# Gates, taps, conv tiles and output products at other items of the attention of two layers

## What is computed

```python
proj = einsum('bld,de->ble', h, w_in[l])
a, g, zc, q, k, v, za, qi, ki, wi = split(proj)
u = a * sigmoid(g)                          # 512 channels
u = depthwise_conv(u, w_dw, width=31) + b_dw
y_conv = silu(layer_norm(u, ln_g, ln_b)) * silu(zc)
y_attn = sparse_attention(q, k, v, qi, ki, wi, topk) * silu(za)   # 8 heads of 64
y = einsum('ble,ed->bld', concat([y_conv, y_attn]), w_out[l])
h = layer_norm(DEEPNORM_ALPHA * h + y, post_ln_g[l], post_ln_b[l])
```

## Time and profile before

| | us |
|---|---|
| median of three runs | 1079.3 (1077.6 to 1079.58) |
| the profiled execution's own time | 1078.45 |
| span of the profiled execution | 1076.7 |
| TensorE busy | 1002.7 |
| VectorE busy | 665.8 |
| ScalarE busy | 582.3 |
| GpSimd busy | 197.1 |

### The profile page before, as it was taken

One profiled execution on the slowest core, in us unless ns is written; L12 is line 12 of the kernel. 1 busy time (PEld: TensorE's weight loads), 2 busy tenths in 40 slices (PEclk: granted clock), 3 DMA queues, 4 the chain that ended last, 5 costly groups with the idle time before them and its releaser, 6 DMA issues.

```text
span 1076.7 us, 16592 instructions
## 1 busy us (share of the span) xinstructions
PE 1002.7 (93%) x6452; PEld 845.7 (79%) x6452; DVE 665.8 (62%) x1507; ACT 582.3 (54%) x944; POOL 197.1 (18%) x236
## 2 busy tenths in 40 slices
PE   6999999987899899999999787889999899999997
PEld 6998988864567799898887466778888778887885
DVE  3899999884673479999978645635631433332422
ACT  6585872555533458588255733444564656664321
POOL 0000661011211100077100302223200000000001
PEclk9999999996999999999999998989999999999999
DMA  7776873760202858487474610594777553547661
GB/s 286 184 175 197 192 175 111 186 155 24 58 1 80 189 149 193 118 186 172 117 179 109 156 36 1 157 232 120 185 172 210 137 118 96 140 122 152 156 157 79
DMA packets 23822, 152.36 MB, mean 142 GB/s; under 512 B 2865, under 2 KB 3377, under 8 KB 6849
## 3 DMA queue, kind: packets, MB, share of 16 engines
q0 software_dynamic: 9648, 68.75, 34.6%
q1 hardware_dynamic: 14096, 82.55, 21.4%
HBM read 149.20 MB, written 2.10 MB: 141 GB/s over the span
## 4 chain that ended last, share of the span: by engine, by line
PE 58%; DVE 21%; ACT 9%; issue 8%; DMA 3%; POOL 1%; POOLq 0%; DVEq 0%; SPq 0%; ACTq 0%
PE psum_B L1227 16%; PE psum_A L1260 7%; PE psum_A L1227 7%; PE psum_B L1260 6%; DVE score L1759 6%; DVE top L1750 5%; PE psum_A L1409 5%; DVE conv_acc L1704 4%; DMA w_lo<-in_weights 2%; PE psum_A L1620 2%; ACT w_hi L622 2%; PE psum_B L1620 2%; ACT w_lo L623 2%; PE psum_B L1409 1%; PE psum_B L1363 1%
## 5 line engine op out<-in xcount | busy, mean ns | idle before, releaser
L1704 DVE SCALAR_TENSOR_TENSOR conv_acc<-u,vec,conv_acc 128x528 f32<-128x528 f32 (+1 forms) x240 | 173.7, 759 | 3.2
L1041 POOL DMA_DIRECT2D w_lo<-in_weights x67 | 59.6, 889 | 605.5 <-ACT w_lo L623 579.1
L1227 PE MATMUL psum_B<-x_hi,w_hi 128*128 128x264 f32 (+3 forms) x512 | 144.2, 320 | 6.6 <-DVE mlp_lo L2129 3.6
L1227 PE MATMUL psum_B<-x_lo,w_hi 128*128 128x264 f32 (+3 forms) x512 | 141.6, 315 | 0.0
L1227 PE MATMUL psum_B<-x_hi,w_lo 128*128 128x264 f32 (+3 forms) x512 | 141.2, 314 | 0.0
L622 ACT ACTIVATE w_hi<-w_raw 128x2048 fp32r<-128x2048 f32 (+2 forms) x85 | 129.3, 1522 | 15.4 <-DMA w_raw<-in_weights 15.0
L623 ACT ACTIVATE w_lo<-w_raw 128x2048 fp32r<-128x2048 f32 (+2 forms) x85 | 128.7, 1514 | 0.0
L1227 PE MATMUL psum_A<-x_hi,w_hi 128*128 128x264 f32 (+2 forms) x496 | 115.9, 291 | 1.4 <-DVE x_lo L1911 1.0
L1227 PE MATMUL psum_A<-x_hi,w_lo 128*128 128x264 f32 (+2 forms) x496 | 113.8, 287 | 0.0
L1227 PE MATMUL psum_A<-x_lo,w_hi 128*128 128x264 f32 (+2 forms) x496 | 113.8, 287 | 0.0
L1227 PEld LDWEIGHTS psum_B<-x_hi,w_hi 128*128 128x128 f32 (+1 forms) x512 | 87.5, 185 | 16.2 <-issue 9.8
(11 more groups left out here) (339 smaller groups left out, 2175.6 us busy)
## 6 DMA issues: line engine op xcount, KB each, us to landing
w_raw<-in_weights SPq DMA_DIRECT2D x67, 1024.0 KB, 5.2
w_lo<-in_weights POOLq DMA_DIRECT2D x65, 1024.0 KB, 8.7
x_first<-in_x_t SPq DMA_DIRECT2D x4, 528.0 KB, 7.1
h<-in_x SPq DMA_DIRECT2D x1, 2048.0 KB, 10.8
out<-h SPq DMA_DIRECT2D x4, 512.0 KB, 2.6
post_ln_g<-in_post_ln_g SPq DMA_DIRECT2D x2, 512.0 KB, 3.8
post_ln_b<-in_post_ln_b SPq DMA_DIRECT2D x2, 512.0 KB, 5.3
w_raw<-in_weights SPq DMA_DIRECT2D x2, 288.0 KB, 5.3
```

What stands on the lines that cost most here:

```text
L1041: pool.dma_start(wlo[n % RING][:, 0:width], io["weights"][n, :, 0:width], accum_op=ALU.add) \
L1227: mm = pe.matmul(ps[0:cols, i, 0:b - a], w[wp][:, kt, at:at + cols], x[xp][:, kt, a:b], start=(kt == 0 and wp + xp == 0), stop=(kt == KD - ...
L1704: got = dve.scalar_tensor_tensor(dst, src, w, dst, ALU.mult, ALU.add)
```

## The change

All of it is in the tables and in the place of three operations. The gates keep their order, but items 4 and 6 have two of them, so that the twelve take ten items; the 38 taps take ten items as well. Conv tiles start two items earlier. The conv norm goes from DVE's extra work to a place of its own, between the masks and the scalings of the turn, and the affine step goes from item c + 3 to c + 4. Output products start at item 17 instead of 19, and some later ones move with them, as do both meta pairs, POOL's clearing of their buffer, post norms and splits. The squares' sums get other columns of a tile that becomes eight columns wide. The last products behind the tables (`OUTPUT_CONV_AT`) keep their items.

```diff
+GATE_ITEMS = (0, 1, 2, 3, 4, 4, 5, 6, 6, 7, 8, 9)
 CONV_AT = {
-    0: ((0, 12, "D", "C"), (1, 14, "B", "C"), (2, 16, "D", "C"), (3, 18, "B", "C"), (4, 20, "D", "C")),
+    0: ((0, 10, "D", "C"), (1, 12, "B", "C"), (2, 14, "D", "C"), (3, 16, "B", "C"), (4, 18, "D", "C")),
...
 OUTPUT_AT = {
-    0: ((19, 0, 0, "A"), (21, 0, 1, "B"), (24, 1, 0, "A"), (25, 1, 1, "B"), (27, 0, 2, "A"), (30, 1, 2, "A"),
+    0: ((17, 0, 0, "A"), (19, 0, 1, "B"), (23, 1, 0, "A"), (24, 1, 1, "B"), (27, 0, 2, "A"), (29, 1, 2, "A"),
         (35, 0, 3, "A")),
-    1: ((19, 0, 1, "A"), (21, 0, 2, "B"), (23, 1, 1, "A"), (25, 1, 2, "A"), (29, 0, 3, "A")),
+    1: ((17, 0, 1, "A"), (19, 0, 2, "B"), (21, 1, 1, "A"), (23, 1, 2, "A"), (27, 0, 3, "A")),
-META_AT = ((18, "attn"), (19, "conv"))
-POST_AT = {0: ((0, 26), (1, 30), (2, 34)), 1: ((1, 26), (2, 28))}
+META_AT = ((16, "attn"), (16, "conv"))
+POST_AT = {0: ((0, 26), (1, 28), (2, 34)), 1: ((1, 22), (2, 26))}
 SPLITS_AT = {
-    0: ((0, 1, ("zc", 2)), (2, 3, ("wo", 0, 0)), (6, 7, ("wo", 1, 0)), (10, 11, ("wo", 0, 1)), (19, 21, ("wo", 1, 1))),
-    1: ((0, 1, ("zc", 2)), (2, 3, ("wo", 0, 0)), (6, 7, ("wo", 1, 0)), (10, 11, ("wo", 0, 1)), (16, 18, ("wo", 1, 1))),
+    0: ((0, 1, ("zc", 2)), (2, 3, ("wo", 0, 0)), (5, 6, ("wo", 1, 0)), (8, 9, ("wo", 0, 1)), (19, 19, ("wo", 1, 1))),
+    1: ((0, 1, ("zc", 2)), (2, 3, ("wo", 0, 0)), (5, 6, ("wo", 1, 0)), (8, 9, ("wo", 0, 1)), (17, 17, ("wo", 1, 1))),
-TAPS_BY_ITEM = (3, 3, 3, 3, 3, 3, 3, 3, 4, 4, 3, 3)
+TAPS_BY_ITEM = (4, 3, 4, 3, 5, 4, 5, 4, 3, 3)
-        todo["dve"][i + 2].append(("norm", t))
+        todo["dve_early"][i + 2].append(("norm", t))
         todo["pe"][i + 3].append(("back", t, back))
-        todo["act"][i + 3].append(("affine", t))
+        todo["act"][i + 4].append(("affine", t))
-        todo["pool"][17].append(("clear", 0))
+        todo["pool"][14].append(("clear", 0))
...
                         masked_logits(l, i + 2)
                         masked_logits(l, i + 3)
+                        for op in early[i]:
+                            conv_norm(l, op[1])
                         normalise(l, i + 2)
                         normalise(l, i + 3)
```

More of the change, by code:

```diff
@@ L195 @@
 CONV_AT = {
-    0: ((0, 12, "D", "C"), (1, 14, "B", "C"), (2, 16, "D", "C"), (3, 18, "B", "C"), (4, 20, "D", "C")),
-    1: ((1, 12, "D", "C"), (2, 14, "B", "C"), (3, 16, "D", "C"), (4, 18, "B", "C")),
+    0: ((0, 10, "D", "C"), (1, 12, "B", "C"), (2, 14, "D", "C"), (3, 16, "B", "C"), (4, 18, "D", "C")),
+    1: ((1, 10, "D", "C"), (2, 12, "B", "C"), (3, 14, "D", "C"), (4, 16, "B", "C")),
 }
 OUTPUT_AT = {
-    0: ((19, 0, 0, "A"), (21, 0, 1, "B"), (24, 1, 0, "A"), (25, 1, 1, "B"), (27, 0, 2, "A"), (30, 1, 2, "A"),
+    0: ((17, 0, 0, "A"), (19, 0, 1, "B"), (23, 1, 0, "A"), (24, 1, 1, "B"), (27, 0, 2, "A"), (29, 1, 2, "A"),
         (35, 0, 3, "A")),
-    1: ((19, 0, 1, "A"), (21, 0, 2, "B"), (23, 1, 1, "A"), (25, 1, 2, "A"), (29, 0, 3, "A")),
+    1: ((17, 0, 1, "A"), (19, 0, 2, "B"), (21, 1, 1, "A"), (23, 1, 2, "A"), (27, 0, 3, "A")),
 }
-META_AT = ((18, "attn"), (19, "conv"))
-POST_AT = {0: ((0, 26), (1, 30), (2, 34)), 1: ((1, 26), (2, 28))}
+META_AT = ((16, "attn"), (16, "conv"))
+POST_AT = {0: ((0, 26), (1, 28), (2, 34)), 1: ((1, 22), (2, 26))}
 OUTPUT_CONV_AT = {0: 39, 1: 31}
@@ L236, in attention_extras @@
     n = len(attention_items(l))
-    todo = {engine: [[] for _ in range(n)] for engine in ("pe", "act", "dve_middle", "dve", "pool")}
+    todo = {engine: [[] for _ in range(n)] for engine in ("pe", "act", "dve_early", "dve_middle", "dve", "pool")}
     for gate in GATES_AHEAD[2:]:
         todo["dve"][0].append(gate)
-    for i, gate in enumerate(GATES_AT):
+    for i, gate in zip(GATE_ITEMS, GATES_AT):
         todo["pe"][i].append(gate)
@@ L371, in build @@
         nmax = sb("neg_max", [P, 4])
-        psums = sb("prob_sums", [P, 4])
+        psums = sb("prob_sums", [P, 8])
         rsums = sb("prob_rsums", [P, 4])
@@ L807, in squares @@
                     act.wait_ge(exp_made.sem, exp_made.at((2, "in", t - 1)))
-                act.activation(dst[:, :], h[:, t, :], ACT.Square, accum_out=psums[:, t - 1:t]) \
+                act.activation(dst[:, :], h[:, t, :], ACT.Square, accum_out=psums[:, t + 3:t + 4]) \
                     .then_inc(exp_made.mark((2, "in", t)), 1)
@@ L1082, in input_deviation @@
                 pool.wait_ge(exp_made.sem, exp_made.at((2, "in", t)))
-                reciprocal_deviation((2, "in", t), psums[:, t - 1:t], 1, P, 8 + t, 1.0 / D, EPS)
+                reciprocal_deviation((2, "in", t), psums[:, t + 3:t + 4], 1, P, 8 + t, 1.0 / D, EPS)
             pool.memset(u[:, :, 0:PAD], 0.0).then_inc(set_up.mark("pad"), 1)
@@ L1947, in _ @@
                 conv(l, 62, TAPS_AHEAD)
-                middle, todo = extras[l]["dve_middle"], extras[l]["dve"]
+                early, middle, todo = extras[l]["dve_early"], extras[l]["dve_middle"], extras[l]["dve"]
                 n = len(items[l])
@@ L1958, in woven @@
                             conv_stats(l, op[1])
-                        elif op[0] == "norm":
-                            conv_norm(l, op[1])
                         elif op[0] == "residual":
```

## The result

The changed kernel takes 1061.68 us (median of 4 runs, 1060.74 to 1063.52), the kernel before 1079.44 (1077.6 to 1082.58): the ratio is 0.9835, with a 95% interval of 0.9808 to 0.9862. The forecast was 1058, range 1047 to 1070. A second set of 6 runs gives 1061.72, ratio 0.9847 (0.9815 to 0.988). All ratios here are to the kernel before, in the same set. The span of the profiled execution goes from 1076.7 to 1059.4 us.

What follows compares the result with a forecast made beforehand. PE bounds the gate stages, a loop of waits across engines the conv stages; output stages hold idle PE and lost clock. Layer 0 gives -10.6, layer 1 -10.3, together -20.9 from 1078.45: 1057.5, said as 1058 us, range 1047 to 1070.

Steps and rivals of the forecast that it cites:

- the named waits: PE's waits: 5.60 us ahead of layer 0's first output product, 3.71 and 4.44 in layer 1's outputs; to shrink or go.
- Conv stages, -9.1 and -5.5: First conv transposes to first output product: 15.5 us instead of 24.60 in layer 0, 17.6 instead of 23.10 in layer 1.
- a loop in which no y and no affine is due yet: Conv stage loop of mask, exponential, scalings and attention y, statistics: 3.9 us, in layer 0 taken as 3.7.
- by PE's work alone: Lower bound of the conv stages from PE's busy time: 15.6 us in layer 0, 15.8 in layer 1.
- the ring: Conv stage loop of waits across engines, 8.0 us for a pair of items in layer 1, to shorten to 6.0.
- The norm: Conv norm between masks and scalings, where DVE idles 2.27 us; its 0.72 us leaves the conv stage's loop.
- rival A: Early norm stops DVE waiting for rstd, 1.8 us for each of four tiles: 1067.5 us; chance 0.22.
- The affine step: An item later, it uses back transposes of the loop before; affine and tanh, 2.07 us, stay in the 6.0 us ring.
- Gates, -2.2 and -2.8: Gate stages of layers 0 and 1: one pair of items less ahead of the first conv transposes saves 2.2 and 2.8 us.
- a sign of being wrong: In the profile after: gate stages as long as before, with zc or taps as releaser.
- Outputs: Output stages, products from item 17: one more pair of items, fewer waits; +0.7 us in layer 0, -3.7 and +1.7 in layer 1.
- rival B: Better than the sum: denser PE leaves no half-clock stretch, layer 1's output waits stay at their floor: 1051 us; chance 0.20.

Runs made afterwards that it cites:

- e5: Changed kernel with two weight splits earlier, halves at items 4, 5 and 6, 7 instead of 5, 6 and 8, 9: 1071.91 us, ratio 0.9921.
- e6: Changed kernel with the second half of the split of w_out's third block at item 10 instead of 9: 1059.17 us; repeated, 1060.95 us.
- e3: Changed kernel with the conv norm behind the scalings of its turn: 1065.12 us, ratio 0.9868.
- e10: Changed kernel with the split's second half at item 10 and the conv norm behind the scalings: 1061.37 us, ratio 0.9836.
- e8: Changed kernel with the affine step at item c + 3 again: 1069.21 us, ratio 0.9895.
- e1: Changed kernel with its twelve gates one an item, in items 0 to 11: 1067.41 us, ratio 0.9892.
- e7: Changed kernel with gates one an item and the two splits at the items of the kernel before: 1068.75 us, ratio 0.9891.

## Why the forecast held, and where it did not

The direction was right, and the time lies in the range (1061.7 for 1058). The mechanism held in part: the named waits went, and loops got shorter. That the total came so near is partly luck. Gates and conv stages were to give 19.6 us and gave 9.5 in the first profile and 12.2 in the second. The output stages gave 5.8 and 1.4 for a forecast of 1.3, and some 2.5 us came from a stretch of the kernel that the forecast put at nothing and whose time goes with the clock. By its steps:

*Conv stages, -9.1 and -5.5.* The big term was mis-sized, in layer 1 most. Two things fill part of the gap. First, "a loop in which no y and no affine is due yet" was summed as if ACT had only copies and exponentials there. At its head stands a split half, 1.9 us, as it did in the kernel before; the change added `x_hi` ahead of it and put the low part's transfer into `x_lo`'s way. With the split half moved, layer 1's stage is 19.2 us at a clock of 0.91; the forecast was 17.6. With both splits far ahead it is 17.86 (e5). Second, the bound "by PE's work alone" was read from busy times that were themselves at two clocks. PE has 11.0 us of work in layer 0's stage at full clock (e6), and 18.0 at a mean of 0.56; in the latter case PE, not the ring of waits, sets 19.3 us. At a clock of 1.00 the stage took 16.43 us in the changed kernel and 15.86 in e6, near the forecast's 15.5.

*The norm.* Not confirmed as a step. The forecast took its 0.72 us out of the ring and rival A put 1.8 us in; the stages of e3 and e10 show neither, and their times leave 0.4 to 3.4 us open. The sign that the forecast named for A did come: VectorE waits for `rstd` ahead of the early norm, up to 1.84 us in the changed kernel (at 256.57). In layer 1:

```profile
599.08 0.81 DVE L1780 TENSOR_SCALAR conv_normed<-psum_D,meanvar,rstd 128x512 f32<-128x512 f32 x1 [1.18 <-POOL rstd L1054]
```

This delays the scalings, but I read the rows so that these do not end last there: the back transposes behind them stand waiting for the affine step of the tile before (1.22 us at 600.20), which holds bank C.

*The affine step.* Its item is worth 7.5 us (e8), by the place that it leaves at the end of ACT's turn as much as by the ring. The forecast has no term for the former.

*Gates, -2.2 and -2.8.* The stage of layer 0 gave nothing, which the forecast had named as a sign of being wrong, and that of layer 1 -2.2. The cover of PE over DVE was thinner in the dense pairs than I took: PE waits 0.5 to 1.0 us for gates there. With gates one an item e1 and e7 lose 6 to 7 us by their medians; the forecast has no term for that.

*Outputs.* The stages gave -1.1 and -4.7 for +0.7 and -2.0; in the second profile +1.7 and -3.1. The named waits went and came as said. That the clock would be 1.00 was rival B's part, and in the second profile a half-clock stretch came back to both.

The rule of the Trainium skill that the forecast weighed ("TensorE: Matmul & The Clock Gate", "What's actually happening") agrees with the rows in that the clock fell behind a wait: it is 1.00 from 233.60 to 235.80, with the wait of 1.30 us in it, and 0.50 from 235.90 on. Then the rows part from it: PE is busy for 17.00 of 17.00 us at 0.50, and activity did not release the clock in that time. It rose about when the output products began, at 252.89. The same wait of 1.30 us in e3 and in the second profile was followed by stages at 0.90 and 1.00. What decides between them no run here shows.

## What to carry to other kernels

When a reordering takes waits away, list everything that stands at the head of the turn it shortens, what was there already and what did not move with the rest: here moving a split half of 1.9 us took 2.4 of the 4.0 us off by which a stage missed its forecast. Then ask how much of such a gain is waits and how much is clock: here 0.7 and 1.7 us. Read a bound "by work alone" at the clock that the stretch had, and look at two profiles before a stage's time is taken as its length. Slack in one stage (gates two an item) can pay in another, by what it keeps out of it.

## What the runs showed of the hardware

One program, one stage, two executions: a granted clock of 0.56 and 1.00, 19.27 and 16.43 us; and PE stayed at 0.50 for 17.00 us in which its rows show no idle time. A scaling of 128x272 on VectorE that starts when GpSimd's `x_lo` has just begun takes 1.58 us instead of 0.36 to 0.40, and ends about when `x_lo` does (583.37 and 583.21). The Trainium skill, "SBUF — State Buffer", section "SBUF: two separate sides", says that GpSimd and VectorE, the latter in some of its forms, share a pair of ports which one instruction holds for its whole length. The rows agree.
